# One step of a hybrid decoder: output products ordered by column halves, the first expert's rows picked by TensorE products, the tenth weight chunk sent later

## The reference

```
x  = x + merged @ w_out
hn = rms_norm(x) * norm_ffn_g
g  = softmax(hn @ w_route_group + b)        # 4 groups, the best one
e  = (hn @ w_route_expert + b)[group]       # 8 experts of it, the best two
y  = sum over the two: w * ((silu(hn @ w_gate[e]) * (hn @ w_up[e])) @ w_down[e])
return x + y
```

## Time and profile before

| what | us |
|---|---|
| median of 3 runs | 1033.21 (1033.18 to 1034.37) |
| profiled execution, own time | 1037.51 |
| profiled execution, span | 1035.7 |
| PE busy | 903.2 (87%) |
| DVE busy | 365.3 (35%) |
| ACT busy | 224.0 (22%) |
| POOL busy | 85.9 (8%) |
| DMA bytes | 258.46 MB, mean 250 GB/s |

### The profile page before, as it was taken

One profiled execution on the slowest core, in us unless ns is written; L12 is line 12 of the kernel. 1 busy time (PEld: TensorE's weight loads), 2 busy tenths in 40 slices (PEclk: granted clock), 3 DMA queues, 4 the chain that ended last, 5 costly groups with the idle time before them and its releaser, 6 DMA issues.

```text
span 1035.7 us, 11180 instructions
## 1 busy us (share of the span) xinstructions
PE 903.2 (87%) x4299; PEld 507.1 (49%) x4299; DVE 365.3 (35%) x806; ACT 224.0 (22%) x570; POOL 85.9 (8%) x89
## 2 busy tenths in 40 slices
PE   6899799999899999999859999787877788778784
PEld 5454677777678888755423433232332333233331
DVE  4588568767353345534414111111110101111010
ACT  3432354364622100032201111000010100001010
POOL 0100000000000000000011122010111011010111
PEclk9999899999999999999959999989999999999998
DMA  8622212112112228096369999999999999999991
GB/s 309 205 82 85 77 41 84 46 42 82 41 41 81 82 82 275 1 396 284 125 250 405 389 395 394 388 415 395 404 398 406 407 401 408 402 413 397 411 395 47
DMA packets 34095, 258.46 MB, mean 250 GB/s; under 512 B 9000, under 2 KB 12328, under 8 KB 18792
## 3 DMA queue, kind: packets, MB, share of 16 engines
q1 hardware_dynamic: 28000, 244.93, 59.4%
q0 software_dynamic: 6048, 12.89, 4.7%
HBM read 252.46 MB, written 14.58 MB: 258 GB/s over the span
## 4 chain that ended last, share of the span: by engine, by line
PE 55%; DMA 26%; DVE 7%; issue 6%; ACT 4%; SPq 1%; another core or an unknown queue 1%; POOL 0%; POOLq 0%; DVEq 0%; ACTq 0%
DMA arena<-in_w_gu 19%; PE ps L1723 19%; PE ps L1996 12%; PE ps L2015 7%; PE ps L1662 6%; DMA arena<-in_w_ed 5%; PE ps L1880 4%; PE ps L1985 2%; DVE arena L1289 1%; ACT arena L825 1%; DVE a_stat L1315 1%; DMA arena<-in_x_T 1%; DVE arena L1312 1%; DMA hn_rows<-arena 1%; ACT arena L837 1%
## 5 line engine op out<-in xcount | busy, mean ns | idle before, releaser
L1723 PE MATMUL ps<-arena 128*128 128x272 f32 x1120 | 269.4, 397 | 13.4 <-ACT arena L725 5.8
L1996 PE MATMUL ps<-arena 128*64 128x512 f32 x512 | 232.8, 603 | 19.7 <-DMA arena<-in_w_gu 19.5
L1723 PEld LDWEIGHTS ps<-arena 128*128 128x128 f32 x1120 | 209.9, 191 | 65.1 <-ACT arena L725 11.5
L1997 PE MATMUL ps<-arena 128*64 128x512 f32 x512 | 233.0, 603 | 0.0
L2015 PE MATMUL ps<-arena 128*64 128x512 f32 x512 | 134.6, 673 | 57.2 <-issue 44.0
L725 ACT ACTIVATE arena<-ps 128x272 f32<-128x272 f32 (+5 forms) x172 | 77.2, 457 | 401.5 <-PE ps L2015 175.3
L1996 PEld LDWEIGHTS ps<-arena 128*64 128x64 f32 x512 | 67.0, 138 | 156.1 <-issue 123.8
L1521 DVE SCALAR_TENSOR_TENSOR arena<-ps,list_w,arena 64x512 f32<-64x512 f32 x32 | 23.8, 743 | 286.5 <-ACT arena L990 286.5
L2015 PEld LDWEIGHTS ps<-arena 128*64 128x64 f32 x512 | 43.7, 153 | 145.8 <-issue 137.0
L1662 PE MATMUL ps<-arena 128*128 128x512 f32 (+1 forms) x192 | 75.6, 552 | 8.1 <-DMA arena<-in_w_kv 7.1
L685 POOL DMA_INDIRECT out_y<-arena,list_i x32 | 45.6, 1426 | 402.9 <-PE ps L1985 342.7
(11 more groups left out here) (224 smaller groups left out, 692.1 us busy)
## 6 DMA issues: line engine op xcount, KB each, us to landing
arena<-in_w_gu SPq DMA_DIRECT2D x64, 2048.0 KB, 48.6
arena<-in_w_ed SPq DMA_DIRECT2D x32, 2048.0 KB, 51.2
arena<-in_w_pair SPq DMA_DIRECT2D x20, 1024.0 KB, 4.8
arena<-in_x SPq DMA_DIRECT2D x8, 512.0 KB, 8.2
arena<-in_w_q SPq DMA_DIRECT2D x2, 2048.0 KB, 16.5
arena<-in_w_out SPq DMA_DIRECT2D x2, 2048.0 KB, 13.4
arena<-in_x_T SPq DMA_DIRECT2D x4, 512.0 KB, 8.9
out_y<-arena SPq DMA_DIRECT2D x4, 512.0 KB, 7.0
```

The source lines that it names most:

```text
L1723: ins = mm(out, w[:, k, :], tokens[:, k, :], start=k == 0 and q in "127", stop=k == 3, skip_group_check=q not in "127")
L1996: mm(ps[0:C, 2 + s, :], xT[s][:, j, :], w[:, jj, 0, :], start=j == 0, stop=j == JX - 1)
L1997: ins = mm(ps[64:64 + C, 2 + s, :], xT[s][:, j, :], w[:, jj, 1, :], start=j == 0, stop=j == JX - 1)
```

## The change

The output products run in two rounds: all first column halves of the four prompt tiles, then all second halves. Half number h is j in the first round and 4 + j in the second. Each half's eight k's are cut 2, 2, 4, with the turn of the half before behind the first two and its router product behind the next two. The router's first-half sums have their own place in PSUM and are copied out and scaled ahead (`part_logits`); the second half's are added in `choice`. All choices but the sample tile's stand in the second round.

Expert 0's rows are no longer gathered. `hits` makes for each tile a column matrix `pick_at` (for each of the 64 places: is this token it, times the norm's factor), and `pick_rows` multiplies x of the tile by it, eight products for each of the five tiles, added up in a PSUM bank that `clear_rows` has set to zero. GpSimd's gathers begin with expert 1. The first list product for the weights and the counts (`list_weights`) move between the two halves of expert 0's `gate_up`. The sample tile of x gets a place in a constant's area, so that all five x loads go out together. SyncE sends chunk 7 when the first round's products are done, chunk 8 when the second's are, then stores the last tile of `hn_rows` itself, then the last y store, and chunk 9 when the rows of expert 1 have landed.

TensorE, where the output stage ends and expert 0 begins. Before: L1895 is the last turn, L1911 the router, L1931 the lists, L1919 and L1922 the ranks, L1958 the counts, L1966 the weights' list, L1985 the turn of gathered rows, L1996 expert 0.

The core of the diff:

```diff
-        g_share, w_first, w_second = (take(NT) for _ in range(3))
+        g_share, w_first, w_second, first_scale = (take(NT) for _ in range(4))
         def half_no(j, c):
-            return 0 if j == 0 else 2 * j - 1 + c
+            return 0 if j == 0 else (NT - 1) * c + j
...
-            sp.wait_ge(y_start[ORDER[0]], 16)
-            sp.wait_ge(turned, 1)
-            sp.wait_ge(hn_ready, 1)
-            load_x(ORDER[4])
-            for j in range(1, NT):
+            sp.wait_ge(out_ready, half_no(NT - 1, 0) + 1)
+            load_chunk(EARLY)
+            for j in range(1, NT - 1):
                 start_y(j)
-            for n in range(EARLY, N_CHUNK):
-                load_chunk(n)
+            sp.wait_ge(out_ready, half_no(NT - 1, 1) + 1)
+            load_chunk(EARLY + 1)
+            sp.wait_ge(hn_ready, NT)
+            t = ORDER[NT - 1]
+            sp.dma_start(hn_rows[t * P:t * P + ROWS[t], :], xn[(NT - 1) % 2][0:ROWS[t], :]).then_inc(hn_last, 16)
+            start_y(NT - 1)
+            sp.wait_ge(x_full[1], 16)
+            load_chunk(EARLY + 2)
...
-            for j, t in enumerate(ORDER):
+            for j, t in enumerate(ORDER[:NT - 1]):
...
-            pool.wait_ge(hn_out[0], 48)
+            pool.wait_ge(hn_out[0], 32)
             pool.wait_ge(hn_out[1], 32)
-            for t in range(2):
+            pool.wait_ge(hn_last, 16)
+            for t in range(3):
                 pool.wait_ge(y_start[t], 16)
+            pool.wait_ge(xe_ready, 1)
             pool.wait_ge(rows_listed, 1)
-            for e in range(2):
-                gather_x(list_i[:, e:e + 1], e)
+            gather_x(list_i[:, 1:2], 1)
+            gather_x(list_i[:, 2:3], 0)
...
             def choice(j):
+                dve.wait_ge(rstd2_ready, j + 1)
+                base = r_bias[0:r, :]
+                if j > 0:
+                    base = part_logits[0:r, t, :]
+                    link(stt(base, base, stat[0:r, 2, t:t + 1], r_bias[0:r, :], ALU.mult, ALU.add))
                 dve.wait_ge(logit_ready, last_half(j) + 1)
...
+                dve.wait_ge(choice_ready, j + 1)
+                ts(first_scale[0:r, t:t + 1], one_hot_bf[0:r, t, 0:1], stat[0:r, 2, t:t + 1], None, ALU.mult)\
+                    .then_inc(pick_scaled, 1)
...
             def hits(j):
                 dve.wait_ge(rank_ready, j + 1)
+                dve.wait_ge(pick_scaled, j + 1)
+                ts(pick_at[t][0:r, :], cc("place")[0:r, :], ps[0:r, 7, t * NE:t * NE + 1], first_scale[0:r, t:t + 1],
+                   ALU.is_equal, ALU.mult).then_inc(picked, 1)
...
             for j in range(1, NT):
                 add_out(j, 0)
-                choice(j - 1)
                 half_mean(j)
+                if j == 1:
+                    choice(0)
+                if j == 3:
+                    hits(0)
+            for j in range(1, NT):
                 add_out(j, 1)
...
                 inverse2(j)
-                hits(j - 1)
-            choice(NT - 1)
+                if j > 1:
+                    hits(j - 1)
+                choice(j)
             hits(NT - 1)
+            dve.wait_ge(hn_out[1], 32)
+            take_x(0, 0)
             dve.wait_ge(list_ready, 1)
...
-            for j in range(1, NT):
-                half_out(j, 0, 0)
-                turn(2 * j - 2)
-                half_out(j, 0, 1)
-                route(2 * j - 2)
-                if j > 1:
-                    tile_list(j - 2)
-                half_out(j, 1, 0)
-                turn(2 * j - 1)
-                half_out(j, 1, 1)
-                route(2 * j - 1)
-                tile_ranks(j - 1)
+            def pick_rows(j, *js):
+                t = ORDER[j]
+                r = ROWS[t]
+                pe.wait_ge(picked, j + 1)
+                rows = x[t][0:r, :].rearrange("c (p j) -> c j p", j=JX)
+                for jj in js:
+                    ins = mm(ps[:, 0, jj * C:(jj + 1) * C], rows[:, jj, :], pick_at[t][0:r, :], start=False, stop=True,
+                             skip_group_check=True)
+                return ins
+            for h in range(1, 2 * NT - 1):
+                half_out(h, (0, 1))
+                turn(h - 1)
+                half_out(h, (2, 3))
+                if h > NT + 1:
+                    tile_ranks(h - NT - 1)
+                route(h - 1)
+                half_out(h, (4, 5, 6, 7))
...
+                if h == 7:
+                    tile_list(1)
+                    clear_rows()
+                    pick_rows(0, 0, 1, 2, 3)
+            pick_rows(0, 4, 5, 6, 7)
             turn(2 * NT - 2)
+            tile_ranks(NT - 2)
+            pick_rows(1, 0, 1, 2)
             route(2 * NT - 2)
...
+            pick_rows(3, *range(JX))
             tile_ranks(NT - 1)
+            pick_rows(NT - 1, *range(JX)).then_inc(xe_ready, 1)
             tile_list(NT - 1)
...
             def step(e, k, half, more, last=False):
+                if isinstance(e, int) and e == 0:
+                    gate_up(0, 0, up_no(0, 0), 0)
+                    turn_x(1, 1, 16)
+                    return
```

More of the change, by code:

```diff
@@ L215, in build @@
         d_probs = area(11968, 4, 256)
-        w_out = area(0, KD, D)
+        w_out = [area(4096 * c, KD, 512) for c in range(2)]
         x_at = [area(8192 + s * D, D) for s in range(4)]
-        x = [x_at[0], x_at[1], x_at[2], x_at[3], x_at[3]]
+        x = x_at + [const[:, CONST["cos"][0]:CONST["cos"][0] + D]]
+        pick_at = [const[:, CONST["before"][0] + t * C:CONST["before"][0] + (t + 1) * C] for t in range(NT)]
+        zero_row = area(50304 + (NT - 1) * (NG + NE), P)
         pick = area(12288, 2, NT, 2, NE)
         hit = area(12928, 2, NT, C)
-        xn = [area(at, D) for at in (13568, 48256)]
+        xn = [area(at, D) for at in (48256, 13568)]
         w_route = area(14592, KD, NG + NE)
@@ L582, in load_x @@
                 sp.dma_start(x[t][0:ROWS[t], :], a["x"][t * P:t * P + ROWS[t], :]).then_inc(x_again[t], 16)
-            for t in ORDER[:4]:
+            for t in ORDER:
                 load_x(t)
@@ L935, in square @@
                 act.wait_ge(x2_ready, half_no(j, c) + 1)
-                above(act, hn_out[j % 2], 16 * (j // 2))
+                above(act, hn_out[j % 2], 16 * (j // 2 if c == 1 else 1 - j % 2 if j else 0))
                 act.activation(xn[j % 2][0:r, cols], x[t][0:r, cols], ACT.Square, accum_out=ssq[0:r, c, t:t + 1])\
@@ L1905, in route @@
                     pe.wait_ge(x2T_last, 1)
-                j, c = (h + 1) // 2, (h - 1) % 2
+                j, c = half_of(h)
                 t = ORDER[j]
-                above(pe, logits_taken, j)
-                for k in range(KD) if h == 0 else range(4 * c, 4 * c + 4):
-                    rows = dec_x2T[:, k, :] if h == 0 else x2T[c][:, k % 4, :]
-                    ins = mm(ps[0:ROWS[t], 6, t * 36:(t + 1) * 36], rows, w_route[:, k, :], start=k == 0, stop=k == KD - 1)
+                above(pe, logits_taken, j if c == 1 else 1)
+                if h >= NT:
+                    pe.wait_ge(first_logits, 1)
+                at = 36 * t if c == 1 else 36 * (NT + t)
+                ks = range(KD) if h == 0 else range(4 * c, 4 * c + 4)
+                for k in ks:
+                    rows = dec_x2T[:, k, :] if h == 0 else x2T[(h - 1) % 2][:, k % 4, :]
+                    ins = mm(ps[0:ROWS[t], 6, at:at + 36], rows, w_route[:, k, :], start=k == ks[0],
+                             stop=k == ks[-1])
                 ins.then_inc(logit_ready, 1)
@@ L1938, in _, with clear_rows @@
             dec_out()
-            for j in range(1, NT):
-                half_out(j, 0, 0)
-                turn(2 * j - 2)
-                half_out(j, 0, 1)
-                route(2 * j - 2)
-                if j > 1:
-                    tile_list(j - 2)
-                half_out(j, 1, 0)
-                turn(2 * j - 1)
-                half_out(j, 1, 1)
-                route(2 * j - 1)
-                tile_ranks(j - 1)
+            def clear_rows():
+                pe.wait_ge(zero_row_set, 1)
+                pe.wait_ge(x2_ready, half_no(1, 1) + 1)
+                for q in range(4):
+                    mm(ps[:, 0, q * P:(q + 1) * P], zero_row[0:1, :], ident[0:1, :], start=True, stop=True)
@@ L1959, in _ @@
-            ins.then_inc(count_ready, 1)
             def list_rows(out, first, n):
@@ L1968, in list_rows, with list_weights @@
                 ins.then_inc(list_ready, 1)
-            pe.wait_ge(hit_ready, NT + 1)
-            list_rows(ps[0:C, 4, 0:NE], 1, 1)
+            def list_weights():
+                for t in range(NT):
+                    r = ROWS[t]
+                    ins = mm(ps[:, 7, 256:256 + NE], ones_bf[0:r, :], one_hot_bf[0:r, t, :], start=t == 0, stop=t == NT - 1)
+                ins.then_inc(count_ready, 1)
+                pe.wait_ge(hit_ready, NT + 1)
+                list_rows(ps[0:C, 4, 0:NE], 1, 1)
             def before_transposing(sem, value):
@@ L1998, in gate_up @@
                     ins.then_inc(used, 1)
```

(2 more changed lines are left out.)

79 lines of the change are left out of this document (48 added, 31 removed).

## The result

| | us |
|---|---|
| before, median of 4 | 1033.79 (1033.18 to 1035.58) |
| the change, median of 4 | 1046.24 (1042.86 to 1048.48) |
| ratio | 1.0106, 95% interval 1.0078 to 1.0135 |
| the change, profiled execution | 1044.43, span 1042.2 |

The change makes the kernel about 1.1% slower, where 0.6% faster was forecast, and the time lies outside the range of 1021.6 to 1031.6. The executions that were profiled show less of it: that of before took 1037.51 us, 3.7 above its median, and that of the change 1044.43, 1.8 under. Of the runs further down, one execution of e5 took 3712.58 us, with matmuls several times their usual length; it was the profiled one, and its trace is not used.

A forecast was written before the change was run, and what follows sets the result against it. The weight-chunk stream was taken as the bound, restarting when chunk 10 goes at 540.59. Chunk 9 11.9 us earlier, less 5.5 (extra chunk 5.2, gather 0.3), nets 6.4 off the 1033.21 median: 1026.8 us, range 1021.6 to 1031.6.

The forecast's parts named there:

- its restart: Expert stage: chunk 9 goes at 528.7, 11.9 us before the 540.6 of before, against 5.5 for added transfers.
- the gather's 2.9: Expert 1's rows: the gather takes 2.9 us, the least of 32 gathers, and lands at 528.6.
- the store's landing before it is wanted: Last hn_rows store on SyncE's queue behind chunk 8: lands at 521.5, wanted at 524.8, slack 3.3 us.
- The last product's end: End of the output stage: last product ends at 512.8 instead of 509.88, with 0.5 added for VectorE's lateness.
- the first tile's four picks: Ahead of the last output product's end: four picks add 0.55 us, half of eight turns' 1.09.
- From the last product to expert 0: Between output and expert stages: 512.8 + 1.3 + 0.69 + 7.2 + 2.6 gives expert 0 at 524.6, before 535.2.
- eight picks 1.05: Last tile's picks ahead of expert 0: 1.05 us, priced by eight turns of a gathered block.
- C: Expert 1's rows come late through a slow store and gather, landing at 536.9 or 541.2: 1035 to 1039.3; chance 0.08.
- B's two mechanisms: VectorE sets the second round's pace (up to 2.5 more) or the gather takes 7.6: 1029 to 1031.5; chance 0.17.
- D: Picks wait for something read as early, expert 0 starts near 530, chunk 10 at 535.4: 1028 to 1029.5; chance 0.05.
- signs of being wrong: Chunk 9 after 535, expert 1's gather 7 us or more, adds over 2 us late, DMA share under 0.9 at 530-550.
- A: Expert stage: the extra chunk costs nothing, TensorE and not the stream counts; 1021.3 to 1022.6 us; chance 0.10.

The follow-up runs named there:

- e5: The kernel before, with chunks 8 and 9 sent only when expert 1's rows have landed; 1035.45 us, ratio 0.9987 to the kernel before.
- e4: The change without its picks, expert 0's rows gathered as in the kernel before; 1032.73 us, ratio 0.9966 to the kernel before.
- e6: The change with the picks' operands exchanged (64-column matrix stationary, x moving 512 wide), no clearing, list written earlier; 1031.19 us, ratio 0.9948 to the kernel before.
- e1: The change with picks taking 128 adjacent columns of x instead of every eighth, weights and gains laid out to match; 1040.13 us, ratio 1.0036 to the kernel before.
- e3: The change with the tenth chunk sent right behind the ninth, no wait for expert 1's rows; 1041.69 us, ratio 1.0055 to the kernel before.
- e2: The change with only the even four of each tile's eight picks, for timing alone; 1035.60 us, ratio 0.9994 to the kernel before.
- e10: A second run of e5's kernel (the kernel before with chunks 8 and 9 late), for a trace; 1035.52 us, ratio 0.9982 to the kernel before.

## Why the prediction was wrong

**Right.** The stream of chunks as the bound, and its restart as the moment that counts: the change's span follows from 540.88 and one more chunk within 0.7 us. By the same sum (the restart, 5.5 for each chunk more than before had left at 540.59, and what stands behind that moment in before) the spans of the nine usable traces of the experiments come out 0.1 to 3.6 us too low, and two pairs change places (e4 and e6, e1 and e3); it misses most for e4 (3.6) and e3 (2.9), where the stream breaks again later. Also right were the 0.9 from list to gather (536.96 to 537.93) and the gather's 2.9 (537.93 to chunk 9 at 540.88), expert 0's first half (5.4; 536.92 to 542.49), the store's landing before it is wanted, the unbroken stream behind the restart (shares of 0.99 and more from 545 on). VectorE was late by little in the second round: the last add began 1.15 us behind its product, 1.3 forecast.

**Right by luck.** The last product's end, 512.8 forecast and 513.56 measured, and with it the last add (514.1 and 514.71). The first output product started 0.84 us earlier in this trace than in that of before (441.67 and 442.51), so the stage grew by 4.5 us and not by 2.9. The excess is the first tile's four picks (1.85 for 0.55) and the clearing (1.08 for 0.60), the same error as below in small.

**The step that failed** is in "From the last product to expert 0": "eight picks 1.05", with its smaller copy ahead of the last product, and the picks of the three tiles between, which the sum put at nothing. It measured 4.08. Two factors of two were missed. The row that I took (eight turns in 1.09) is of transposes, which are one instruction each in these traces, while a float32 product is two; the row of the router's products (eight instructions for four products) said so. And with every eighth column as the stationary operand a part takes 0.25 us at full clock, where a strided transpose took 0.13 and a router part with adjacent columns 0.13. No row of before that the prediction read shows a strided stationary load in a two-part product, and I should have bounded the pick's price from the router's rows at 1.8 us at least; instead I gave it no upper end.

**What followed from it.** The sum had no term at all for the picks of the three tiles between the first and the last; I took them as lying beside VectorE's choice. At 4.05 each they don't fit beside it: the picks of the change hold TensorE from 516 to 531, the last router product and with it the choice come 1.3 us late beyond the 0.6 of the adds, and the ranks another 7.5, so that they are 9.4 late in all. The last pick adds 3.0. These are, to a tenth, the 12.3 us between 524.6 and 536.92, and 540.88 instead of 528.7 is the same 12.2 passed on. The experiments that halve the picks or exchange their operands take it back: chunk 9 at 531.90 and 527.57.

**Of the rivals** none was this one. C had the right side and, by luck, nearly the right moment (541.2 as its far end), by a mechanism that did not occur, and its time (1035 to 1039.3) is still 7 us short: in the change the last store took 4.5 us and the gather 2.9. B's two mechanisms did not occur either: VectorE did not set the pace, and the gather took 2.9. D named late picks, for another reason, and priced them at 2 us. Of the signs of being wrong, a chunk 9 behind 535 and DMA shares under 0.9 from 530 on came true; they were meant as signs of a late gather or a full ring, and neither was the cause. A is refuted by the change itself: an expert 0 that starts 1.7 us later, with the stream's restart only 0.3 later, costs 6.5 us of span, because of the extra chunk. The lesson for the range is that the new operation whose duration no row showed was the one with no bounds in it.

## What to carry to other kernels

Price a small matmul by its stationary load and count its parts: for narrow outputs exchange the operands so that the few columns are stationary and the wide rows move. An operation that is put in front of the last link of a chain costs its full length even when its own result is early; look in the order for what stands between a ready operand and the instruction that wants it. Where a prefetch ring sets the end, count idle DMA time up to the last transfer; a transfer that is held back must be paid for by an earlier restart.

## What the runs showed of the hardware that was not expected

- A two-part float32 product with every eighth column stationary: 0.25 us a part at a granted clock of 1.00 (the change at 502.8, e2 at 515.71) and of 0.50 (the change at 532). With adjacent columns: 0.13 and 0.23 (e1; the router's products). A transpose with the same stride, from 64 rows: 0.14 at 1.00 (before at 543.91, eight in 1.09).
- In the change TensorE is busy for 5.00 of 5.00 us in each window from 515 to 530, with weight loads for 4.7 to 4.8 of them. The granted clock falls to 0.50 (the lower level, 1.2 GHz) between 516.5 and 517, while the picks run, and stays there until expert 0's 512-column products have run from 536.92 to about 540.5. The Trainium skill (TensorE: Matmul & The Clock Gate, Part 1: The HAM clock gate) says that activity releases the throttle; by the engine's busy time this trace does not agree, since the 13 us from 517 to 530, without a gap in the records, did not bring the clock back.
- A store of 512 KB that was issued while a 2 MB chunk was moving landed about 1 us behind that chunk, on either queue: on GpSimd's, 9.2 us after its issue, the chunk 11.2 after its own (e10: 521.3 and 520.7); on SyncE's queue behind the chunk, 4.5 and 7.8 (the change: 522.7 and 521.4). Behind two chunks on SyncE's queue it took 9.8 (e3). The store of e10 was issued 2.6 us after its chunk and that of the change 4.6 us, so these runs don't show that one queue is better than the other.
- A table load of 1.28 us ahead of a silu, between two groups of products, went with a granted clock of 0.54 in the five microseconds after it in e4, and of 0.66 in the change, e2 and e6. But before (load at 544.10) and e10 (537.78) have the same load and a granted clock of 1.00 behind it, so the load alone does not bring the clock down.
